# A two-layer attention and convolution backbone on one core: value products of four heads in one piece, a third weight block ahead of the first shift, and one variance sum moved to VectorE

## The reference

```python
h = modulate(rmsnorm(x, g_mix[l]), sh1, sc1)
hc = modulate(rmsnorm(ctx, g_mix[l]), csh1, csc1)
q, k, v, u = split_in(h @ w_in[l])
...
a_out = latent_attention(q, k, v, k_ctx, v_ctx, sink)
cv_out = conv_module(u, w_dw[l], b_dw[l], ln_g[l], ln_b[l])
x = x + gt1 * merge_groups(a_out, cv_out, g_attn_out[l], g_conv_out[l], w_out[l])
h2 = modulate(rmsnorm(x, g_ffn[l]), sh2, sc2)
x = x + gt2 * swiglu(h2, w_gate_up[l], w_down[l])
```

## Time and profile before

| | us |
|---|---|
| median of 3 runs | 1522.55 |
| lowest and highest of the 3 | 1519.5, 1524.03 |
| the profiled execution, whole | 1523.91 |
| its span in the trace | 1522.1 |
| TensorE busy | 1492.6 |
| VectorE busy | 891.8 |
| ScalarE busy | 529.0 |

### The profile page before, as it was taken

One profiled execution on the slowest core, in us unless ns is written; L12 is line 12 of the kernel. 1 busy time (PEld: TensorE's weight loads), 2 busy tenths in 40 slices (PEclk: granted clock), 3 DMA queues, 4 the chain that ended last, 5 costly groups with the idle time before them and its releaser, 6 DMA issues.

```text
span 1522.1 us, 22743 instructions
## 1 busy us (share of the span) xinstructions
PE 1492.6 (98%) x8962; PEld 1231.3 (81%) x8962; DVE 891.8 (59%) x1335; ACT 529.0 (35%) x810; POOL 104.5 (7%) x149
## 2 busy tenths in 40 slices
PE   8999999999999999999999999999999999999998
PEld 5766776688888888888888889777689888888887
DVE  4756779677667325765853466768887433333334
ACT  4302368634222112222122244138844322222234
POOL 0133200040000000000000000520030000000000
PEclk9999999999999999999999999999999999999999
DMA  9493600023332123323432123520023333333322
GB/s 375 167 263 96 237 27 29 1 70 111 119 143 96 56 91 144 124 110 138 154 109 69 45 67 111 150 64 15 29 70 98 97 96 97 97 96 97 97 83 97
DMA packets 40855, 161.15 MB, mean 106 GB/s; under 512 B 5584, under 2 KB 6992, under 8 KB 34640
## 3 DMA queue, kind: packets, MB, share of 16 engines
q1 hardware_dynamic: 36848, 148.72, 29.0%
q0 software_dynamic: 3936, 11.45, 2.8%
HBM read 149.76 MB, written 2.10 MB: 100 GB/s over the span
## 4 chain that ended last, share of the span: by engine, by line
PE 89%; DVE 6%; issue 2%; DMA 2%; ACT 1%; SPq 0%; ACTq 0%; DVEq 0%
PE banks L624 75%; PE banks L653 3%; PE banks L800 2%; PE banks L787 2%; PE banks L815 2%; PE banks L536 1%; DMA ada_raw<-in_w_ada 1%; PE banks L679 1%; DVE neg_max L1445 1%; PE banks L545 1%; DVE ada_sum_context L1412 0%; DVE x L1421 0%; PE banks L589 0%; DMA ada_first<-in_w_ada_first 0%; PE banks L853 0%
## 5 line engine op out<-in xcount | busy, mean ns | idle before, releaser
L624 PE MATMUL banks<-h_both,w_high 128*128 128x258 f32 (+2 forms) x2432 | 492.9, 324 | 4.2 <-DVE tmp L1373 1.7
L989 ACT ACTIVATE w_high<-raw 128x1024 fp32r<-128x1024 f32 (+2 forms) x182 | 186.2, 1023 | 706.5 <-PE banks L624 645.7
L624 PEld LDWEIGHTS banks<-h_both,w_high 128*128 128x128 f32 x2432 | 364.3, 189 | 51.8 <-issue 15.1
L1327 DVE TENSOR_TENSOR w_low<-raw,w_high 128x1024 fp32r<-128x1024 f32 (+2 forms) x182 | 216.4, 1189 | 246.9 <-ACT w_high L989 243.5
L624 PE MATMUL banks<-h_both,w_low 128*128 128x512 f32 (+1 forms) x1216 | 293.7, 323 | 0.0
L624 PEld LDWEIGHTS banks<-h_both,w_low 128*128 128x128 f32 x1216 | 187.2, 189 | 17.7
L624 PE MATMUL banks<-h_normal_low,w_high 128*128 128x512 f32 x304 | 118.3, 389 | 0.0
L624 PE MATMUL banks<-h_normal_high,w_high 128*128 128x512 f32 x304 | 118.3, 389 | 0.0
L624 PE MATMUL banks<-h_normal_high,w_low 128*128 128x512 f32 x304 | 118.3, 389 | 0.0
L1372 DVE COPY shift_product<-banks 128x2 f32<-128x2 f32 x78 | 12.3, 158 | 169.3 <-PE banks L624 160.2
L624 PE MATMUL banks<-ff_high,w_high 128*128 128x512 f32 x352 | 90.2, 337 | 0.0
(11 more groups left out here) (218 smaller groups left out, 2058.6 us busy)
## 6 DMA issues: line engine op xcount, KB each, us to landing
raw<-in_w_gu SPq DMA_DIRECT2D x88, 512.0 KB, 3.5
ada_raw<-in_w_ada SPq DMA_DIRECT2D x20, 1024.0 KB, 5.6
raw<-in_w_dn SPq DMA_DIRECT2D x32, 512.0 KB, 3.5
raw<-in_w_mix SPq DMA_DIRECT2D x28, 512.0 KB, 4.6
ada_in_ff<-in_w_ada SPq DMA_DIRECT2D x12, 1024.0 KB, 5.6
raw<-in_w_out SPq DMA_DIRECT2D x16, 512.0 KB, 3.5
ada_first<-in_w_ada_first SPq DMA_DIRECT2D x7, 1024.0 KB, 11.9
raw<-in_w_dn SPq DMA_DIRECT2D x16, 384.0 KB, 3.0
```

Of the source, the lines that this page charges most:

```text
L624: last = mm(bank[:, 2 * slot + bk, to:to + b - a], weights[w][:, k0_w + k, :], rhs[:, k0_rhs + k, a:b], start=(k == 0 and n == 0), stop=(k ...
L989: last = f(wH[j][:, at, :], raw[j][:, at, :], ACT.Copy)
L1327: last = tt(wL[j][:, at, :], raw[j][:, at, :], f32(wH[j][:, at, :]), ALU.subtract)
```

## The change

Six things are changed. (1) `values` runs all key tiles of a group behind unit 1 of the next group. (2) A third block's latents run before the first shift: `w_first` holds block 0's split weights, so that both `wH`/`wL` pairs are free for blocks 1 and 2; block 2 uses banks 6 and 7 for this; the root's broadcast and token rows of the start go to bank 5. (3) In the prologue SP loads three pairs of scale units ahead of the first weight block, the fourth pair in two halves, and the third weight block ahead of the last shift pairs; the ten `keep_busy` matmuls between and behind the scale units become four. (4) The shift's columns are made after the context's squares, once and not in two places; ScalarE and VectorE do all eight context tiles before the squares. (5) Five units of modulation group 1 are loaded into five buffers as soon as the shift's units have run, and `at` moves unit 1 one block earlier, unit 3 and units 5 and 6 too. (6) In layer 1 VectorE adds the squared tiles, and root and `diagonal` stand ahead of the split of block 4's weights.

```diff
-        first_in = [sem(f"ada_first_in{j}") for j in range(DT)]
+        first_in = [sem(f"ada_first_in{j}") for j in range(DT + 1)]
...
-                at = (2, 3, 3, 4, 5, 6, 6, 7)
+                at = (2, 2, 3, 3, 4, 5, 6, 7)
...
+        for k, (tile, landed, count, free) in enumerate((
+                (ada_raw[:], ada_in[0], 16, DT), (ada_in_u[:], ada_in[1], 16, DT), (zr_flat[1], ada_more[0], 16, DT),
+                (zr_flat[0], ada_more[1], 16, DT), (ada_in_cv[:], ada_more[2], 16, DT),
+                (ada_raw[:], ada_in[0], 32, DT + 1), (ada_in_u[:], ada_in[1], 32, DT + 2), (ada_raw[:], ada_in[0], 48, DT + 6))):
+            ADA_PLACES[1, k] = (tile, landed, count, (ada_mm, free))
...
+            for p in range(3):
+                load_half(0, p)
+            load_first(0)
             sp.dma_start(ident[:], ident_in).then_inc(const_in, 16)
-            load_first(0)
-            load_half(0)
+            load_half(0, 3)
...
             load_first(1)
-            load_half(1)
+            load_half(1, 0)
+            load_half(1, 1)
+            sp.wait_ge(w_low, 1)
+            sp.dma_start(raw[0][:].rearrange("p k m -> p (k m)"), w_mix[0, 0, 1]).then_inc(raw_in[0], 16)
...
+            load_half(1, 2)
+            load_half(1, 3)
...
+            for k in range(5):
+                load_ada((1, k))
...
                         for m in range(len(qs[q][2])):
-                            if m * GRP // len(qs[q][2]) == n % GRP:
+                            if n % GRP == 1:
                                 values(q, m)
...
                 if k in (1, 3, 5):
-                    keep_busy(3)
-            keep_busy(1)
+                    keep_busy(2 if k == 1 else 1)
...
+            pe.wait_ge(rs_ok, 1)
             first_turn(1)
             keep_busy(2)
...
+            for u in ada_units(0, "u", 2):
+                ada_unit(u)
+            gemm_block(0, "u", 1, 1, DT, hH, hL, mod_cols(True))
+            for u in ada_units(0, "u", 3):
+                ada_unit(u)
...
             sum_done("x", 0, DT)
             diagonal((0, "n1"), NB)
-            first_columns(0, ada_tr).then_inc(ada_cols, 1)
-            dve.wait_ge(ada_cols, 1)
...
             for k in range(DT):
                 low(k, k, x[:, k, :], gains(0, 0, True, k)[1:])
+            for k in range(DT):
                 add_square("xc", 0, k, L, N)
             sum_done("xc", 0, DT, N)
+            chain.link(first_columns(0, ada_tr))
+            nc.vector.tensor_copy(shiftsH[1], mod[:, 0, 0:DT, :]).then_inc(sh_high, 1)
```

More of the change, by code:

```diff
@@ L400, in token_rows, with turned_roots @@
         def token_rows(key, blocks):
[L402 to L404 removed]
+            first = BC if key[1] == "var" else SMALL if key in ((0, "n1"), (0, "n1c")) else ADA
+            return wide[:, 512 * first:512 * first + P * blocks]
+        def turned_roots(key, blocks):
+            first = SMALL if key in ((0, "n1"), (0, "n1c")) else BC
+            return wide[:, 512 * first:512 * first + P * blocks]
         def token_mean(key):
@@ L604, in stat_broadcast @@
                         pe.wait_ge(rs_ok, rs_index[key[0], "cn"] + 1)
-                    for b in range(first_block(key), first_block(key) + blocks):
-                        last = nc.tensor.transpose(wide[:, 512 * BC + P * b:512 * BC + P * b + P],
-                                                   per_tok[:, 1, b:b + 1].to_broadcast([P, P]), ident[:])
+                    for b in range(blocks):
+                        c = b + first_block(key)
+                        last = nc.tensor.transpose(turned_roots(key, blocks)[:, P * b:P * b + P],
+                                                   per_tok[:, 1, c:c + 1].to_broadcast([P, P]), ident[:])
                     last.then_inc(bc_ok, 1)
@@ L1168, in _ @@
                 for t in range(V_TILE):
+                    if t == 2 and not context:
+                        root((layer, "var"), blocks)
                     split_high(layer, "qkv", t // 2, t % 2)
@@ L1173, in _ @@
                             f(cv[:, k, 0:width], z[:, k, 0:width], ACT.Square).then_inc(dev_ok, 1)
-                    if t == 2:
+                        f(psums[:, 0:1], eps[:], ACT.Sqrt)
+                    if t == 2 and context:
                         root((layer, "var"), blocks)
@@ L1636, in u_pair @@
                     dve.wait_ge(gemm, 2 * use + 1)
-                    scale_product(0, context)
+                    scale_product(0, context, BC // 2 if (layer, i) == (0, 1) else 0)
                     if i:
@@ L1669, in _ @@
                         scale_deviation(layer, width)
+                    if t == 2 and not context:
+                        diagonal((layer, "var"), blocks)
                     split_low(layer, "qkv", t // 2, t % 2)
+                    if t == 1 and not context:
+                        for k in range(1, CT):
+                            dve.wait_ge(dev_ok, CT * layer + k + 1)
+                            made = tt(ssum[:, 0:width], ssum[:, 0:width] if k > 1 else cv[:, 0, 0:width],
+                                      cv[:, k, 0:width], ALU.add)
+                            if k < CT - 1:
+                                chain.link(made)
+                        made.then_inc(conv_sum, 1)
                     if t > 1:
```

160 lines of the change are left out of this document (95 added, 65 removed).

## The result

| | before, us | with the change, us |
|---|---|---|
| median | 1522.18 (8 runs, 1519.5 to 1526.61) | 1531.78 (8 runs, 1530.49 to 1534.98) |
| the profiled execution, whole | 1523.91 | 1531.5 |
| its span in the trace | 1522.1 | 1529.7 |

The changed kernel takes 1.0059 times as long, with a 95% interval of 1.0048 to 1.0071: some 9 us slower. The forecast was 1525, no difference that can be told; the measured 1531.78 is at the very end of its range, just past the 1531.5 that its text names, where the slower rival stood (1530.7), and outside the 1520 to 1529.5 of the forecast itself.

A forecast was written before the change was run, and what follows sets the result against it. Bound in attention: TensorE and ScalarE's loop through banks 4 and 5. 1523.91 - 8.1 (prologue) + 10.9 (attention) - 0.2 (variance) = 1526.5, less 1.36 for the median: 1525; own bounds 1520 to 1531, 8-in-10 range 1511 to 1531.5.

The forecast's parts named there:

- What bounds the kernel: Prologue: loads, scale units and h_both; attention: TensorE and ScalarE looping through banks 4 and 5; layer 1's qkv: VectorE.
- the attention term: Both layers' attention: gathering the values loses 10.9 us, 5.6 in layer 0 and 5.3 in layer 1; bounds 8 to 13.
- the rule on mode switches: Attention: mode switching requires a drain, so saving 48 pieces at 0.25 us each would bring the full 12.0 us.
- the plain group: Attention, four units, no extra ScalarE step: 8.4 us now, 8.8 with the change, so 0.4 slower.
- unit-by-unit working: Attention, three engines followed: 82.2 us in layer 0 unchanged (trace 81.4); the change adds 5.6 there, 5.3 in layer 1.
- 0.05 of signalling: Attention, loop through banks 4 and 5: signalling beside 0.86 start and 0.70 copy, making the loop 1.6 us.
- rival C: Units 8 to 21, both layers: ScalarE's idle time not made good, attention 13.6 lost, prologue 5.5 gained; 1530.7; chance 0.20.
- The prologue: Start to convolution: 4.5 us from block 3, 1.0 from a unit, 2.6 from a wait; 8.1 gained, bounds 5.5 to 9.
- that fall: Prologue, thin stretch at 41 to 45 us: granted clock might drop to 1.2 GHz, a case for the 5.5 gain bound.
- Layer 1's variance: Layer 1: three VectorE adds against GpSimd slowdown and per_tok wait; 0.2 us gained, bounds 1.5 gained to 2.3 lost.
- The sum: Whole kernel: 1523.91 - 8.1 + 10.9 - 0.2 = 1526.5 for the profiled execution, forecast median 1525, bounds 1520 to 1531.
- A: Attention comes out even, as ScalarE and VectorE run ahead behind the value piece; prologue gain stays; 1514.5; chance 0.22.

The follow-up runs named there:

- e2: The kernel before, with only a group's value tiles put in one piece behind unit 1 of the next group; 1539.31 us beside 1521.83.
- e3: The changed kernel, with ScalarE copying only the first key tile of the transposed probabilities from each layer's fifth group on; 1523.86 us.
- e4: The kernel before, with ScalarE copying only the first key tile of the transposed probabilities from each layer's fifth group on; 1520.1 us beside 1523.25.
- e1: The changed kernel with the value tiles spread over the four units again (the spread variant); 1517.59 us beside 1521.83 for the kernel before.
- e9: e6 with six more result-less keep_busy steps in TensorE's idle stretches at the start; 1513.33 us, ratio 0.9935 to the kernel before.
- e10: The kernel before, with unit 6 of modulation group 1 behind block 7 instead of block 6 of u; 1522.14 us beside 1522.96.
- e8: e6 with layer 1's variance sum on GpSimd again, and root and diagonal behind the split; 1514.77 us.
- e6: e1 with the shift's row copied after the second context square and its columns made after the fourth add; 1514.28 us.
- e11: e9 with a group's values in one piece behind unit 1; 1529.09 us.
- e7: e6 with a group's values in two pieces, behind units 1 and 3; 1522.76 us.

## Why the prediction came out as it did

**What bounds the kernel, and the sign of the attention term: right.** TensorE was 98% busy, and less work on it made the kernel slower. The loop through banks 4 and 5 was there as the rows before showed it, the value piece was its filling (e2, e3, e4), and the rule on mode switches changed nothing in that: each end of a piece costs what I read, since the 3.73 us unit is 0.68 + 0.58 + 0.16 + 2.31 by its rows, and 2.31 is five tiles of 0.43 and 0.16 for leaving. The Trainium skill, page "TensorEngine Tiling (Array Packing)", has this drain ("Mode switching requires drain"), and the trace agrees; 48 of them were saved and nothing came of it, because in an uneven order the time between pieces isn't TensorE's. With the copy shortened it is TensorE's, and there the plain groups come out 0.3 and 0.2 us shorter (e3, e4).

**The attention term's size: too small, 10.9 for 13.4 to 13.8.** The step that failed is the plain group: "three of them and the longer one, 2.43, are 3x1.99+2.43 = 8.4 a group". No group of the trace without a `conv_norm` step is like that. Units of 1.99 us have scores of 384 columns and one value tile each, four to a group: 7.95 (units 28 to 31). The group that has five value tiles has its scores in 256 columns, and takes 2.26+1.82+1.82+1.83 = 7.73 (units 32 to 35). With the change these groups take 8.57 and 8.82, and 8.8 was the forecast. So the group after was right and the group before was put too long, and the losses are 0.62 and 1.08 us, not 0.4. The same shows in my unit-by-unit working, which gave 82.2 us for the attention as it is and not 81.4: this is 0.8 of the 2.0 us by which layer 0's loss, 7.6, goes beyond my 5.6.

A second number was wrong, the "0.05 of signalling": from the end of the copy to the next transposes are 0.14 us (267.73+0.71 to 268.58), so that the empty unit is 1.69 and not 1.6, and my bound of 0.08 was too low as well. In the plain group it is made up for: three empty units are 0.27 longer, and the unit with all the values is 3.73 where I had 3.98. What it adds to the whole, no run tells. The largest losses are 1.4 and 1.7 us, in the groups whose units have four key tiles (units 12 to 15 and 36 to 39), where most value tiles had cost nothing; the prediction shows no working for a group of that kind. Units 8 to 21 lost 2.5 us together by e2's trace of layer 0, near the 0.3 to 1.3 a group that I had given them, and units 28 to 47, where ScalarE has no `conv_norm` step, lost 4.5. So rival C had the price right, 13.6, and the wrong place: ScalarE's extra steps aren't what went beyond the forecast.

**The prologue: most steps right, but it gives 5.7 where I had 8.1.** Block 3 starts at 58.42, outside the 54.5 to 57.5 that the prediction had set as its sign. Loads and scale units came 0.8 us later than I put them, and the context parts 0.9 later (45.76 for 44.9). The wait ahead of them is there, 2.31 us for some 2.5, but it is for ScalarE's row and not for VectorE: the row stands behind ScalarE's eight squares, and the last square waits 0.54 us for one of VectorE's adds. From there to block 3 I had 11.1 us, e1 has 11.1, and the changed kernel 12.7: the 1.5 us are the clock's. I had that fall as a bound of this term, and as a part of rival C; it belonged in the sum as likely: of the three traces that have this prologue unaltered, the changed kernel's and e3's have it and e1's doesn't. The row on which I leaned for it is weak support: the fall begins at 1513, and TensorE's busy time at 1512 to 1514 is 1.78 of 2 us, hardly "little to do". That six `keep_busy` steps fewer cost nothing is neither confirmed nor refuted: e9 adds as many, and is 0.9 us faster. Behind block 3 the other 3.6 us came as forecast, 1.0 for the unit and 2.6 for the wait, though that wait is worth only 0.8 in the medians (e10). That the whole gain of the start reaches attention was right: 5.70 at the convolution, 5.71 at the first transposes. That it comes from the third block and not from the loads alone wasn't tested apart. By medians the rest of the change is worth 4.2 us (e1), 3.2 to 7.3 by its interval, which is less than the 6.8 by which the two traces differ at layer 0's first transposes. The profiled execution of before lay 1.4 us above its median, and about 1 of it lies between the two attentions: nine other traces need 750.1 to 750.5 us there, this one 751.5; e9's needs 751.1, and those of e4 and e10, which lose the clock there, 751.2 and 753.8. Where the rest of the difference is, the runs leave open.

**Layer 1's variance: right within what can be told.** 0.2 us gained was the forecast; the traces of e1 and e8 give 0.3 between the attentions, the medians of e6 and e8 0.5, and neither is clear of the noise.

**The sum.** By the cuts of the two traces it is 1523.91 - 5.7 + 8.9 - 1.2 + 5.8 - 0.2 = 1531.5, as measured. Of the 8.9, 1.3 are the fall of the clock at 237 us, and 0.3 of the 1.2 are the variance. For such an execution the forecast was 1526.5, so 5.0 us are to be explained. The prologue gave 2.4 less, 1.5 of them by the fall of the clock; the two attentions lost 14.7 for 10.9, which is 3.8 more, 1.3 of them by the clock. Against these 6.2 us stand the 1.2 gained between the attentions. The range of the sum's own bounds was also added up wrong: 1522.55 - 5.5 + 13 + 2.3 is 1532.4 at the slow end, not 1531. That the total came out near C's 1530.7 is in part luck, since C had the losses in another place. The rival on the faster side, A, had supposed that the other engines run ahead behind the value piece. They don't: in the changed kernel ScalarE's copies wait 21.7 us in this attention for TensorE, against 13.3 before, and the longest of these waits, 2.4 us, is as long as a value piece:

```profile
ACT probT L1144 <- PE banks L840: 21.7, 31, 2.4
```

## What to carry to other kernels

When an engine alternates with another through one buffer, count that loop first, with all four parts of it: work, start-up, copy, and the way back. Here the work of the fast engine that fitted in the loop's slack was free or nearly so, though it was cut into pieces with a drain at each end, and gathering it into one piece made it cost its full length while the slack stayed empty. Read the group as it is from the rows of that very group before you take a difference: 8.4 for 7.7 to 8.0 us was the larger error here. And look at which instruction a small copy stands behind: the shift's steps moved ahead of most of the squares were worth 2.3 us by the traces, 3.3 by the medians.

## What the hardware showed beyond that

The granted clock can fall behind waits that are short. In the traces it went to the 1.2 GHz level at 8 to 14, 15 to 23, 46 to 49, 102 to 106, 237 to 243, 288 to 292 and at several places from 1021 to 1046 us, for 3 to 8 us each, and near the end of every trace. Where the rows show what TensorE did before, it had waited 0.6 to 2.4 us at a time. But such a wait doesn't always bring the fall: behind 2.42 us of waiting for unit 6 the clock fell in e2, and behind 2.60 us at the same place it stayed up in the kernel before; behind the 2.31 us ahead of the turn it fell in the changed kernel, and behind 2.32 us it stayed up in e1. Over whole executions it can be read from the mean granted clock: the changed kernel took 1530.5 us at a mean of 0.999 and 1534.4 at 0.995, the spread variant 1516.2 and 1518.9, so 0.7 to 1 us for each thousandth; e10's eleven runs, from 0.995 to 1.000, show no such slope. Two single traces can therefore differ by a few us that no edit has made. The Trainium skill, page "TensorE: Matmul & The Clock Gate", describes in its section on a second failure mode that short idle stretches between groups of matmuls which cycle through PSUM banks let the clock swing. Layer 0's attention agrees as far as it goes: between its first and last transposes the clock falls in two of four traces with the single piece, and in none of eight with the values spread. In layer 1's attention it falls in one of those four (e11), in e7 and in one of the eight (e9), so whether the single piece makes it likelier stays open.
